# The hybrid trunk's step on one core: stores of the cumulated decays in two transfers, the fifth late weight group issued ahead of them, and x read back in two transfers

## What is computed

```
mod   = silu(c) @ ada_w + ada_b                       # six groups of 1024: shifts, scales, gates; c and c_ctx
h     = rmsnorm(x) * (1 + sc_m) + sh_m
proj  = h @ w_in                                      # xbc, z, dt, hgrn inputs, gate logits
y_ssd = ssd(conv_silu(xbc), softplus(dt), ...) @ w_ssd_out     # 8 groups of 4 heads, chunks of 128, both ways
y_hg  = hgrn2(...) @ w_hgrn_out                                # 8 heads, both ways
x     = x + g_m * ((gate_1 * y_ssd + gate_2 * y_hg) @ w_out)
h     = rmsnorm(x) * (1 + sc_f) + sh_f
x     = x + g_f * ((silu(h @ ffn_w1) * (h @ ffn_w3)) @ ffn_w2)
y     = rmsnorm(x) * norm_final_w
```

## Time and profile before

| what | value |
| --- | --- |
| median of three runs | 3158.39 us (3157.52 to 3159.66) |
| the profiled execution | 3156.18 us, span 3154.4 us |
| TensorE matmuls busy | 98% of the span |
| VectorE, ACT, GpSimd busy | 49%, 39%, 24% |
| mean granted TensorE clock | 0.990 of full |

### The profile page before, as it was taken

How to read it: one execution, slowest core, us unless ns; L and a number is a source line. 1 busy time by engine, 2 the same in 40 slices (tenths; PEclk the granted TensorE clock), 3 DMA queues, 4 the chain that set the end, 5 groups by cost and what they waited for, 6 DMA issues and landing times. The chain is left out here.

```text
span 3154.4 us, 59753 instructions
## 1 busy us (share of the span) xinstructions
PE 3075.8 (98%) x22180; PEld 2949.0 (93%) x22180; DVE 1542.1 (49%) x2645; ACT 1221.1 (39%) x2319; POOL 751.5 (24%) x935
## 2 busy tenths in 40 slices
PE   6999999999999999999999989999999999999998
PEld 4799999999999999999999979998989999999998
DVE  3546846567466574674656323444262222222234
ACT  6336455455454555645545432211241101110122
POOL 0014535345243462353524500000200000000002
PEclk8999999999999999999999999999999999999999
DMA  7522222122221221222212334434111111111112
GB/s 257 208 90 72 80 66 91 47 76 84 64 89 40 80 79 53 72 84 67 84 47 75 97 123 137 138 108 128 47 37 44 40 40 41 46 40 47 40 34 87
DMA packets 291346, 250.61 MB, mean 79 GB/s; under 512 B 10936, under 2 KB 262944, under 8 KB 291104
## 3 DMA queue, kind: packets, MB, share of 16 engines
q1 hardware_dynamic: 257024, 197.07, 20.3%
q10 hardware_dynamic: 34080, 50.35, 5.0%
HBM read 210.90 MB, written 36.47 MB: 78 GB/s over the span
## 5 line engine op out<-in xcount | busy, mean ns | idle before, releaser
L749 PE MATMUL bank<-h_hi,w_hi 128*128 128x384 f32 (+1 forms) x2520 | 877.4, 348 | 9.4 <-DVE w_lo L1369 9.4
L749 PE MATMUL bank<-h_hi,w_lo 128*128 128x384 f32 (+1 forms) x2520 | 845.1, 335 | 0.0
L749 PE MATMUL bank<-h_lo,w_hi 128*128 128x384 f32 (+1 forms) x2520 | 844.5, 335 | 0.0
L2066 PE MATMUL bank<-a_hi,v_hi 128*128 128x384 f32 x1440 | 486.2, 338 | 22.2 <-DVE v_lo L2288 11.1
L749 PEld LDWEIGHTS bank<-h_hi,w_hi 128*128 128x128 f32 (+1 forms) x2520 | 472.7, 188 | 26.5 <-DVE w_lo L1369 9.5
L2066 PE MATMUL bank<-a_lo,v_hi 128*128 128x384 f32 x1440 | 483.4, 336 | 0.0
L2066 PE MATMUL bank<-a_hi,v_lo 128*128 128x384 f32 x1440 | 483.2, 336 | 0.0
L749 PEld LDWEIGHTS bank<-h_lo,w_hi 128*128 128x128 f32 (+1 forms) x2520 | 473.3, 188 | 4.0
L749 PEld LDWEIGHTS bank<-h_hi,w_lo 128*128 128x128 f32 (+1 forms) x2520 | 472.4, 187 | 1.4
L1847 POOL TENSOR_TENSOR kq<-kq,fg 128x384 f32<-128x384 f32 x288 | 290.3, 1037 | 176.6 <-PE bank L878 141.6
L2066 PE MATMUL bank<-b_hi,v_hi 128*128 128x384 f32 x912 | 306.6, 336 | 8.0 <-DVE v_lo L2288 8.0
(11 more groups left out here) (270 smaller groups left out, 4222.3 us busy)
## 6 DMA issues: line engine op xcount, KB each, us to landing
raw<-in_w_in SPq DMA_DIRECT2D x104, 512.0 KB, 4.1
cumb<-cum_scratch SPq DMA_DIRECT2D x72, 512.0 KB, 5.9
raw<-in_ffn_w SPq DMA_DIRECT2D x60, 512.0 KB, 3.9
ada_late<-in_ada_w SPq DMA_DIRECT2D x8, 2048.0 KB, 8.4
small<-gate_scratch ACTq DMA_DIRECT2D x72, 192.0 KB, 2.4
gate_scratch<-th ACTq DMA_DIRECT2D x48, 192.0 KB, 1.9
y_scratch<-x_t SPq DMA_DIRECT2D x8, 1152.0 KB, 4.8
small<-y_scratch ACTq DMA_DIRECT2D x48, 192.0 KB, 2.5
```

Source lines behind the costliest of these rows:

```text
L749: last = pe.matmul(out, w[i][:, k, 0:cols_n], h[:, k, blk(hb)], start=(k == 0 and j == 0), stop=(k == KT - 1 and j == 2))
L2066: last = pe.matmul(banks[3 * s + b][:, 0:BW], wp[s][:, k, :], operand[ap][:, k, blk(b)], start=(k == 0 and j == 0), stop=(k == kt - 1 and ...
```

## The change

Four edits.

1. `cum_scratch` is laid out as [chunk][direction][group][head][token]. One transfer per direction stores all nine chunks (32 partitions x 9 pieces of 512 bytes), two in place of eighteen, and the waits on `cum_stored` count two.
2. `load_cum` reads two pieces of 2 KB, one for each direction, in place of one of 4 KB.
3. The fifth late weight group, `load_ada(8)`, stands ahead of the wait for `cum_done` and of the stores. Groups 9 and 10 each move up by one place in the loop behind them.
4. x comes back in two transfers with a semaphore each: tiles 0 and 1, then tiles 2 to 7. VectorE waits for the first only, in the iteration i = 0, which is written out ahead of the loop; later iterations wait for both.

```
@@ -159,7 +159,7 @@
         banks = [ctx.enter_context(nc.psum_tensor(f"bank{i}", [P, 512], F32)) for i in range(8)]
         y_dram = nc.dram_tensor("y_scratch", [24, P, T], F32, kind="Internal").ap()
         gate_dram = nc.dram_tensor("gate_scratch", [16, P, T], F32, kind="Internal").ap()
-        cum_dram = nc.dram_tensor("cum_scratch", [G, NC, 2, HPG, P], F32, kind="Internal").ap()
+        cum_dram = nc.dram_tensor("cum_scratch", [NC, 2, G, HPG, P], F32, kind="Internal").ap()
         x_dram = nc.dram_tensor("x_scratch", [KT, P, T], F32, kind="Internal").ap()
         ident, ones = cst[:, K_ID:K_ID + P], cst[:, K_ONE:K_ONE + P]
 
@@ -633,8 +633,9 @@
 
                 if c >= 3:
                     sp.wait_ge(m_ready.sem, m_ready.at(g, c - 2))
-                src = cum_dram[g:g + 1, c] if isinstance(g, int) else cum_dram[bass.ds(g, 1), c]
-                sp.dma_start(cumb[:, c % 3, :], src.rearrange("a d h t -> a (d h t)").broadcast_to([P, 8 * P])
+                src = cum_dram[c, :, g:g + 1] if isinstance(g, int) else cum_dram[c, :, bass.ds(g, 1)]
+                sp.dma_start(cumb[:, c % 3, :].rearrange("p (d n) -> p d n", d=2),
+                             src.rearrange("d a h t -> a d (h t)").broadcast_to([P, 2, HPG * P])
                              ).then_inc(cum_in[c % 3], 16)
 
             def stage_a(g):
@@ -677,19 +678,19 @@
                 load_ada(t + 2)
                 load(None, t, PRO_COLS[t][0])
             load_ada(7)
+            load_ada(8)
             sp.wait_ge(cum_done, 1)
             for d in range(2):
-                for c in range(NC):
-                    sp.dma_start(cum_dram[:, c, d], cum[32 * d:32 * d + 32, chunk(c)]).then_inc(cum_stored, 16)
+                sp.dma_start(cum_dram[:, d].rearrange("c g h t -> (g h) c t"),
+                             cum[32 * d:32 * d + 32, :].rearrange("p (c t) -> p c t", t=P)).then_inc(cum_stored, 16)
             for t in (5, 6):
                 load(None, t, PRO_COLS[t][0])
-                load_ada(t + 3)
-            load_ada(10)
+                load_ada(t + 4)
             load_ada(11)
             load_a(0, 0)
             load_a(0, 1)
             sp.wait_ge(mod_turned, ADA_N - ADA_FIRST)
-            sp.wait_ge(cum_stored, 16 * 2 * NC)
+            sp.wait_ge(cum_stored, 16 * 2)
             for c in range(3):
                 load_cum(0, c)
 
@@ -1314,7 +1315,7 @@
 
             early, late = range(0, EDGE), range(EDGE, SLOTS)
             ch.round(0)
-            act.wait_ge(cum_stored, 16 * 2 * NC)
+            act.wait_ge(cum_stored, 16 * 2)
             stage_a(0, early, None)
             with act.Fori(0, G - 1) as g:
                 ch.g = g
@@ -1917,7 +1918,7 @@
     unit_done, freed, acc_done = sem("m_unit_done"), sem("m_freed"), sem("m_acc_done")
     small_in = [sem(f"m_small_in{i}") for i in range(6)]
     hi_done, parts = sem("m_hi_done"), sem("m_parts")
-    x_back = sem("m_x_back")
+    x_back = [sem("m_x_back0"), sem("m_x_back1")]
     sq_done, sq_added, sums_zero = sem("m_sq_done"), sem("m_sq_added"), sem("m_sums_zero")
     ms_done, ln_done, rstd_done, t_done = sem("m_ms_done"), sem("m_ln_done"), sem("m_rstd_done"), sem("m_t_done")
     th_done = sem("m_th_done")
@@ -2268,7 +2269,8 @@
                     tail()
                 elif name == "o":
                     act.wait_ge(parts, PARTS["up"])
-                    act.dma_start(x_acc[:, :, :], x_dram.rearrange("k p t -> p k t")).then_inc(x_back, 16)
+                    for i, ks in enumerate((slice(0, 2), slice(2, KT))):
+                        act.dma_start(x_acc[:, ks, :], x_dram[ks].rearrange("k p t -> p k t")).then_inc(x_back[i], 16)
                     with act.Fori(0, n - 1) as i:
                         body(name, i, False)
                     turn()
@@ -2292,7 +2294,9 @@
 
                 t = i * 2 + s
                 if name == "o":
-                    dve.wait_ge(x_back, 16)
+                    dve.wait_ge(x_back[0], 16)
+                    if not isinstance(i, int) or i > 0:
+                        dve.wait_ge(x_back[1], 16)
                 else:
                     dve.wait_ge(freed, done(name, i, s, b) - 1)
                 dve.wait_ge(unit_done, done(name, i, s, b))
@@ -2453,7 +2457,8 @@
                         body(name, i, False)
                     tail()
                 elif name == "o":
-                    with dve.Fori(0, n - 1) as i:
+                    body(name, 0, False)
+                    with dve.Fori(1, n - 1) as i:
                         body(name, i, False)
                     turn()
                 elif name == "up0":
```

## The result

The changed kernel takes 3183.84 us (median of 4 runs, 3181.84 to 3185.05), the kernel before 3158.8 in the same comparison. The ratio is 1.0079, with a 95% interval of 1.0067 to 1.0091: 25 us slower, where 16 us faster was forecast. TensorE's two stalls that the forecast counted on are gone. The loss sits between them, in the rounds of the mixers.

What follows compares the result with a forecast made beforehand. TensorE, busy 98% of the span, was taken as the bound. Removing its two stalls, 7.44 + 8.86 = 16.3 us, from the median 3158.39 us gave 3142.1 us, 0.52% faster, range 3138.5 to 3147.

Steps and rivals of the forecast that it cites:

- stall A: Prologue: TensorE waits for the fifth late weight group, queued behind eighteen stores; moving it ahead saves 7.44 us.
- The sign that failed: Prologue: TensorE's granted clock would be full from 90 to 200 us if the forecast was right.
- stall B: Start of w_out: TensorE waits for a tile's low half behind x's return; splitting x's transfer saves 8.86 us.
- rival 1: Start of w_out: x's two transfers interleave and the first part lands late; 3151.0 us, chance 0.04.
- a rule against this part: x's return: advice to batch transfers of 1 MiB and more would land the second part up to 2 us later.
- two stores for eighteen: Prologue, SP's queue: sixteen fewer issues free 11.4 us, but nobody on TensorE's path waits for them; value 0.
- The read back in halves: Decay loads in the rounds: 2 KB pieces cost 0, between -1.8 and +2 us each, with 4.9 us to hide it.
- Rival 3: Chunk products: halved loads landing over 4.9 us later stop TensorE twice in each of eight groups; 3176 us, chance 0.04.
- Rivals 2 and 4: Prologue gain lost to another stall, 3149.5 us, chance 0.04; both stalls only move, about 3158 us, chance 0.03.

Runs made afterwards that it cites:

- the run with `EDGE = 10`: The changed kernel with the place where the round loop returns to its start moved one slot later, from slot 9: 3142.16 us, ratio 0.9958.
- the 24 KB run: The changed kernel with the old layout order and eighteen stores, but padded so a load's two pieces stand 24 KB apart: 3185.16 us, ratio 1.0083.
- the run with both mends: The changed kernel with the pieces 18 KB apart and the round loop's return one slot later: 3140.07 us, ratio 0.9949.
- the run by itself: The kernel before with only x coming back in two transfers: 3145.57 us against 3156.99, ratio 0.9966.
- old-layout run: The changed kernel with the old layout of the decays, eighteen stores and one 4 KB piece per partition in the read back: 3141.14 us, ratio 0.9953.
- 18 KB run: The changed kernel with one unused group in the decays' layout, so a load's two 2 KB pieces stand 18 KB apart: 3141.49 us, ratio 0.9955.
- the read back alone: The kernel before with only the new layout and the read back in two pieces 16 KB apart, still eighteen stores: 3193.61 us, ratio 1.0118.

## Why the prediction was wrong, step by step

**Right: stall A and its margin.** Forecast 7.4 us, measured 6.6 alone. The group issued at 121.78 (forecast 121.34), the step of 11.16 us held, and the low half of the next tile was in time. The sign that failed is the clock, which was to be full from 90 to 200 us. In 190 to 192 us the kernel after runs at half clock, though TensorE has work throughout; the run with `EDGE = 10` doesn't (its row below):

```profile
188.00:190.00 2.00, 2.00 (x16) 1.46 (x15) 0.31 (x1) 0.23 (x1) 0.00 (x0) 0.88 0.64 155
190.00:192.00 2.00, 2.00 (x7) 2.00 (x7) 0.00 (x0) 2.00 (x6) 0.00 (x0) 0.50 0.67 180
```

```profile
190.00:192.00 2.00, 2.00 (x14) 2.00 (x13) 0.00 (x0) 1.24 (x4) 0.68 (x4) 1.00 0.95 166
```

It follows the many small products and transposes of 186.8 to 189.7 us. Among the profiled executions the clock falls there in nine of the eleven kernels with the early group, and in none of the three without it. It stays full in the first run with `EDGE = 10` and in the 24 KB run, but not in the run with both mends, which has `EDGE = 10` too, so `EDGE` is not what decides. Why it falls stays open; its price can be read. From the start of the first late group to the mark of round 1 the kernel before takes 312.0 us, the two runs at full clock 304.6, which is the forecast 7.4 less, and the nine others 306.1 to 306.4. The fall takes 1.5 to 1.8 us of A's gain, more than the 1 us each way that the forecast allowed for the clock.

**Right: stall B.** Forecast 8.9 us; 8.7 in the trace, 11.4 (7 to 14.5) by itself. In the profile of the run by itself 8.8 us lie behind x's issue; another 2.0 lie ahead of the first late group (95.13 in place of 97.14), where nothing was changed. x's first part took 5.3 us where 5.4 was estimated, and the second 14.2, so the two did not interleave (rival 1). The forecast called the Trainium skill's advice to use transfers of 1 MiB and more ("DMA: Bandwidth & Descriptors", Rule under "Bandwidth") a rule against this part. It is none: the two parts, 1152 and 3456 KB, are both above that size. The second landed 0.2 us later than the whole had, where the forecast gave up to 2.

**Right: two stores for eighteen, value 0.** The old-layout run with eighteen stores and the 18 KB run with two are 0.35 us apart. The issue that the forecast could not see takes 0.86 us for both stores.

**The step that failed: "The read back in halves".** Its value was 0, "so shorter pieces show no penalty, and I take 0", with +2 us for a load as its far end and 4.9 us as its cover. Measured, it costs about 40 us: the changed kernel is 25.0 us slower than the kernel before, the old-layout run 14.7 us faster, each in its own comparison, and the trace shows 42.6 us in rounds 1 to 6. Two things in it were wrong.

First the price. The rows compared the length of pieces, and that comparison was sound: 2 KB pieces 2304 bytes, 4 KB or 18 KB apart cost nothing. What the edit also changed is where the second piece stands, and I read no row for that and gave it no term. At 16 KB the transfer time of a load goes from 1.3 to 3.1 us, near the +2 us bound for one load. But loads stand in queues of three, so the last of them comes some 5 us late.

Then the cover. The margin was taken from who needs the data, in round 0. That round was the wrong place, as it falls into the loop and doesn't return to its start: it takes only 0.2 to 0.3 us longer after the change, by its marks. And the data was the wrong user. What waits behind the loads without a semaphore is the code. The kernel before already said so, at the same point of its round 2 (timelines of VectorE and TensorE):

```profile
664.17 0.69 DVE L1442 TENSOR_TENSOR t_off<-bank,tok_g 128x512 f32<-128x512 f32 x1 [4.38 <-issue]
...
665.67 0.48 PE L792 MATMUL bank<-c_t,b_t 128*128 128x128 f32 x2 [0.31 <-issue]
```

VectorE stopped there for 4.38 us with no releaser, and TensorE for 0.31: the code already came a little late. TensorE had no cover left at this place, where the forecast counted on 4.9 us.

With the loads slow, moving the return by one slot takes the loss away; with the return at slot 9, quick loads take it away. The Trainium skill ("Runtime: NRT & Kernel Launch", Instruction fetch mechanics) says that each engine refills its instruction memory over its own queue in 16 KB blocks, and that a taken branch whose target isn't loaded waits for that transfer. These traces agree: the stops stand at the six returns, the packets of code that move late move just ahead of the end of the stops, and the packets of one of the profile's two instruction queues are 16 KB each (148 for 2.42 MB; the other's are 8 KB). Which engine's code a packet carries the profile doesn't say. That page was not weighed in the forecast.

**Rival 3** had the sign and the place, with a chance of 4%, and the wrong mechanism: it made TensorE wait for the decays, twice in each of eight groups. It stopped once in each of six rounds, and not for the decays. Rivals 2 and 4 did not occur.

**Open.** Why a distance of 8 KB or a multiple costs more than half of the rate was not shown. Two pieces that fall on the same part of the memory, while all 16 engines read the same bytes for 128 partitions, would fit. The late weight groups read 2 KB pieces from rows 24 KB apart and land in 8.5 us for four times the bytes, so the distance alone is not enough; whether it needs the repeated reading was not run. The Trainium skill ("DMA: Bandwidth & Descriptors", Latency and other measured facts) reports rates that fall with large power-of-two row pitches, 207 GB/s at 512 KB, 164 at 2 MB and 103 at 4 MB, and 214 at 4 MB with 4 KB of padding. The padding part agrees here (18 KB is quick); the effect stands at far smaller distances in this kernel, and 24 KB is no power of two.

## What to carry to other kernels

When a transfer's layout changes, cost the distance between its pieces as well as their length, above all where many partitions read the same few pieces; padding the distance from 16 to 18 KB cost nothing here and was worth about 40 us. At each loop's return look at what is in the transfer queues. ACT, VectorE and TensorE waited for code there, and no semaphore and no named wait showed it, only an idle time with releaser "issue". An experiment that changes a layout changes its stores too: look at what they set free before calling the run "the read back alone". Take the margin of a loop from a round that returns to its start. Here the first and the last round were not like the others.

## What the runs showed of the hardware

- Loads of two 2 KB pieces to all 128 partitions ran at 363 GB/s (18 KB apart) or at 167 (16 KB apart), with nothing else changed. By their landings, 5.6 to 6.3 us against 8.0 to 9.0, they are quick at 2.25, 4 and 18 KB and slow at 8, 16, 24 and 32 KB.
- Packets of code use the 16 engines of the data. Of the eight at a return the first moved among the loads, but the second 2 us later in the kernel before and 6 us later in the kernel after, when the loads were nearly through. In the kernel after a stop of ACT and VectorE of 9.6 us and of TensorE of 4.3 us ended behind them. The loads ran 1.8 us longer each.
- The issue of a store of 32 partitions x 512 bytes took 0.66 us where it wrote eight pieces of DRAM apart from each other, and 0.42 us where it wrote one block of 16 KB.
- TensorE's clock can fall without an idle gap: granted 0.50 in 190 to 192 us of the kernel after, behind some 3 us of small products, and full in the same stretch of two other kernels with the same order of work there.
